# A fused encoder block in fp32 on one core: the up projection with the activations stationary and 512 weight columns moving

## The reference

```python
h = rms_norm(x, norm_mix)                 # x: 256 tokens x 2048
proj = h @ w_in                           # attention: a sliding-window group with sinks
...                                       # and a forgetting-attention group
x = x + mixed @ w_o                       # w_o: 2048 x 2048
h = rms_norm(x, norm_ffn)
u = h @ w_up                              # w_up: 2048 x 11264 (gate half, value half)
c = conv_b + sum(pad(u)[:, j:j + S] * conv_w[j] for j in range(3))    # causal, over tokens
gate, val = c[..., :5632], c[..., 5632:]
x = x + (silu(gate) * val) @ w_down       # w_down: 5632 x 2048
out = rms_norm(x, norm_final)
```

## Time and profile before

| | |
|---|---|
| median of 3 runs | 1058.93 us (1058.59 to 1066.37) |
| the profiled execution | 1067.34 us, span 1065.5 us |
| granted TensorE clock, mean | 0.999 of 2.4 GHz |
| TensorE busy | 1055.5 us |
| VectorE, ScalarE busy | 807.4 us, 627.8 us |
| up projection on TensorE | 332.1 to 831.8 us |

### The profile page before, as it was taken

The page is one execution under the profiler, slowest core; times in us unless marked ns, Lnnn a source line. Parts: engine busy times, 40 slices in busy tenths (PEclk is TensorE's granted clock), DMA queues, the critical chain, the costliest instruction groups (busy, mean ns, idle before and its releaser), DMA issues.

```text
span 1065.5 us, 17821 instructions
## 1 busy us (share of the span) xinstructions
PE 1055.5 (99%) x5921; PEld 902.3 (85%) x5921; DVE 807.4 (76%) x1222; ACT 627.8 (59%) x971; POOL 86.8 (8%) x150
## 2 busy tenths in 40 slices
PE   9999999999999999999999999999999999999997
PEld 8888888888888888888888888888888888888885
DVE  5677777676887777777777777766877888876777
ACT  6957575746455655565555556555655666646663
POOL 1000000001011110111111111101111000000000
PEclk9999999999999999999999999999999999999999
DMA  9575655587888898989898888988889688887993
GB/s 295 177 236 168 183 162 177 177 254 193 255 251 250 261 241 271 245 262 243 257 266 242 264 228 274 258 258 239 249 261 251 218 290 292 279 297 268 329 304 113
DMA packets 191493, 259.35 MB, mean 243 GB/s; under 512 B 10820, under 2 KB 140580, under 8 KB 191328
## 3 DMA queue, kind: packets, MB, share of 16 engines
q1 hardware_dynamic: 173776, 215.32, 62.5%
q0 software_dynamic: 17360, 43.22, 18.4%
q10 hardware_dynamic: 320, 0.34, 0.1%
HBM read 256.73 MB, written 44.06 MB: 282 GB/s over the span
## 4 chain that ended last, share of the span: by engine, by line
PE 92%; DVE 4%; DMA 2%; ACT 1%; issue 0%; SPq 0%; DVEq 0%; ACTq 0%
PE pj L1619 16%; PE tr_ps L1619 15%; PE pj L1377 9%; PE pj L1621 8%; PE tr_ps L1621 8%; PE pj L1379 5%; PE pj L1365 4%; PE pj L1367 4%; PE pj L1366 4%; PE sc_ps L1365 4%; PE sc_ps L1367 4%; PE sc_ps L1366 4%; PE pj L1392 3%; DVE split L911 2%; DVE prob L1124 1%; PE pj L1394 1%
## 5 line engine op out<-in xcount | busy, mean ns | idle before, releaser
L911 DVE TENSOR_TENSOR split<-raw,split 128x1024 fp32r<-128x1024 f32 x266 | 321.4, 1222 | 125.9 <-ACT split L593 120.6
L593 ACT ACTIVATE split<-raw 128x1024 fp32r<-128x1024 f32 x260 | 272.0, 1057 | 88.4 <-PE pj L1621 33.1
L1619 PE MATMUL tr_ps<-act_split,split 128*128 128x512 f32 x704 | 250.1, 399 | 0.3 <-DVE act_split L1111 0.3
L1619 PE MATMUL pj<-act_split,split 128*128 128x512 f32 x704 | 249.8, 399 | 0.0
L1621 PE MATMUL pj<-act_split,split 128*128 128x256 f32 x704 | 197.7, 281 | 0.0
L1621 PE MATMUL tr_ps<-act_split,split 128*128 128x256 f32 x704 | 197.7, 281 | 0.0
L1214 DVE TENSOR_TENSOR split<-raw,split 128x1024 fp32r<-128x1024 f32 (+1 forms) x124 | 136.8, 1135 | 38.3 <-ACT split L856 36.3
L1619 PEld LDWEIGHTS tr_ps<-act_split,split 128*128 128x128 f32 x704 | 132.3, 188 | 33.4 <-DVE act_split L1111 0.5
L1619 PEld LDWEIGHTS pj<-act_split,split 128*128 128x128 f32 x704 | 132.3, 188 | 33.4 <-DVE split L911 0.3
L856 ACT ACTIVATE split<-raw 128x1024 fp32r<-128x1024 f32 (+1 forms) x124 | 119.4, 986 | 69.6 <-PE sc_ps L1367 34.7
L1377 PE MATMUL pj<-act_split,split 128*128 128x512 f32 x416 | 147.5, 398 | 0.0
(11 more groups left out here) (243 smaller groups left out, 1525.9 us busy)
## 6 DMA issues: line engine op xcount, KB each, us to landing
raw<-w_up SPq DMA_DIRECT2D x176, 512.0 KB, 5.6
raw<-w_in SPq DMA_DIRECT2D x72, 512.0 KB, 3.8
raw<-w_down SPq DMA_DIRECT2D x68, 512.0 KB, 5.6
t_dram<-w_down POOLq DMA_DIRECT2D x60, 512.0 KB, 6.0
raw<-t_dram SPq DMA_DIRECT2D x40, 512.0 KB, 5.9
raw<-w_o SPq DMA_DIRECT2D x32, 512.0 KB, 5.3
t_dram<-t_dram POOLq DMA_DIRECT2D x40, 256.0 KB, 5.8
raw<-w_down SPq DMA_DIRECT2D x20, 256.0 KB, 5.9
```

Source lines behind the costliest of these rows:

```text
L593: ins = act.activation(hi[:, slot, 0:TILE], raw[:, slot, 0:TILE], ACT.Copy)
L911: dve.tensor_tensor(lo[:, slot, 0:n], raw[:, slot, 0:n], hi[:, slot, 0:n].bitcast(F32), ALU.subtract).then_inc(lo_done, 1)
L1619: pe.matmul(up_banks[v][b], wh[:, c, b * P:(b + 1) * P], act_both(k), start=k == 0, stop=False, skip_group_check=True)
```

## The change

A step of the up projection is now a pair `j` of halves: half `v` = 0 makes 512 gate columns, `v` = 1 the 512 value columns that belong to them. Each half has eight tiles of 2 blocks of input features x 512 columns (`wide`, rows of 2 KB in place of 1 KB). The activations are stationary, and 512 weight columns move, with `mm3` as in the w_o stage, into two banks for the two blocks of tokens; the two halves alternate between two pairs of banks. The result has tokens on the partitions. It is turned in two steps: ScalarE copies each block of 32 partitions to the partitions of the features (`move_blocks`, 16 copies of 32 partitions x 256 elements, in the first three tiles of the next half), and one VectorE transpose of 128 x 1024 turns all 32 x 32 blocks into `ub` (`turn_moved`). Scaling, convolution, SiLU, gate and split follow during tiles 4 to 7 of that next half, with wider instructions for the last four. The addition of two result halves (`up_r`) is gone.

The fourth group of y is now turned by VectorE in squares as the others, in the first tiles of the up projection. `r2b` is filled by two DMAs on ScalarE's queue, a write of the factors to DRAM and a read that spreads them over the partitions. The post-processing of the last half moves into the first six tiles of the down projection, so the sums tiles start later (`SUMS_AFTER`), and the two more raw slots are used from the thirteenth tile on.

```diff
-UP_SPLITS = [[], [4], [5], [6], [], [8], [9], [10]]
-SUMS_AFTER = ((5, 6, 7, 10, 11, 12, 15, 16, 19, 20), (4, 5, 7, 8, 9, 10, 12, 13, 14, 15))
+SUMS_AFTER = ((8, 9, 11, 12, 13, 15, 16, 17, 19, 20), (4, 5, 7, 8, 9, 10, 12, 13, 14, 15))
...
-    return t % RING if t < 2 * RING else (t - RING) % (RING + EXTRA)
+    return t % RING if t < 3 * RING else (t - 2 * RING) % (RING + EXTRA)
...
+MOVES = {0: (0, 6), 1: (6, 11), 2: (11, SIDE * SIDE)}
+def step_of(j, v, per, c):
+    return j * (2 * per) + (v * per + c)
...
+        moved = sb("moved", [P, 4, MT, SIDE, BLOCK])
+        ub = sb("ub", [P, 4, S + 2])
+        conv_o = sb("conv_o", [P, 2, 4, S])
...
         @block.scalar
+            def root_of_squares(s):
+                if s == 1:
+                    act.wait_ge(y2_tot, 1)
+                    act.activation(root2, tot2, ACT.Sqrt, bias=eps, scale=1.0 / D).then_inc(y2_root, 1)
+                if s == 3:
+                    act.wait_ge(r2_s, 1)
+                    act.dma_start(r2_dram.rearrange("m p -> p m"), r2c, allow_slow_non_contiguous=True).then_inc(r2_out, 16)
+                if s == 6:
+                    act.wait_ge(r2_out, 16)
+                    act.dma_start(r2b[:], r2_dram.rearrange("m p -> (m p)").partition_broadcast(P)).then_inc(d_r2, 16)
+            def move_blocks(j, v, first, last, tiles_done):
+                if first == 0:
+                    act.wait_ge(mm_done, tiles_done)
+                    if not (isinstance(j, int) and 2 * j + v == 0):
+                        act.wait_ge(u_s, step_of(j, v, 2, 0))
+                for i in range(first, last):
+                    a, b = divmod(i, SIDE)
+                    rows = up_banks[v][a * BLOCK:(a + 1) * BLOCK].rearrange("p m (w b i) -> p m w b i", w=4, b=SIDE)[:, :, :, b]
+                    ins = act.activation(moved[b * BLOCK:(b + 1) * BLOCK, :, :, a].rearrange("p w m i -> p m w i"), rows, ACT.Copy)
+                if last == SIDE * SIDE:
+                    ins.then_inc(moved_s, 1)
...
+            def finish(j, v, s):
+                if s in MOVES:
+                    move_blocks(j, v, *MOVES[s], step_of(j, v, UP_TILES, T_UP + UP_TILES))
+                if s in (4, 5):
+                    conv_first(j, v, s - 4)
+                if s == 7:
+                    if v == 0:
+                        silu_gate(j)
+                    else:
+                        gated_hi(j)
+            def up_step(j, v, first):
                 for s in range(UP_TILES):
+                    split_hi(step_of(j, v, UP_TILES, T_UP + s + LEAD), (s + LEAD) % RING)
+                    if v == 1:
+                        finish(j, 0, s)
+                    elif not first:
+                        finish(j - 1, 1, s)
...
             for t in range(DOWN_END):
+                if t == 0:
+                    move_blocks(*last_step, 0, half, T_DOWN)
+                if t + LEAD < DOWN_END:
                     down_hi(t + LEAD)
+                if t == 0:
+                    move_blocks(*last_step, half, SIDE * SIDE, T_DOWN)
+                if t == 2:
+                    conv_first(*last_step, 0)
+                    conv_first(*last_step, 1)
+                if t == 5:
+                    gated_hi(UP_PAIRS - 1)
...
         @block.vector
+            def turn_moved(j, v):
+                dve.wait_ge(moved_s, step_of(j, v, 1, 1))
+                st.done(dve.transpose(ub[:, :, 2:S + 2], moved[:].rearrange("p w m a i -> p w (m a i)")))
...
             def up_step(j, v, first):
+                    if not start:
+                        if s == 3:
+                            turn_moved(p, b)
+                        if s == 4:
+                            scale_rows()
+                        if s == 7 and b == 1:
+                            gate(p)
+                    split_lo(step_of(j, v, UP_TILES, T_UP + s + LEAD), (s + LEAD) % RING)
...
+                        if s in (5, 6):
+                            conv_rest(p, b, s - 5)
+                        if s == 7 and b == 1:
+                            gated_lo(p)
...
         @block.tensor
             def up_step(j, v, first):
+                if not first:
+                    pe.wait_ge(moved_s, step_of(j, v, 1, -1))
...
+                    if first and v == 0:
+                        pe.wait_ge(ylo_s, 2 * s + 2)
+                    pe.wait_ge(lo_done, step_of(j, v, UP_TILES, T_UP + s + 1))
+                    wh, wl = wide(hi, s % RING), wide(lo, s % RING)
+                    for c in range(2):
+                        k = 2 * s + c
+                        for m in range(MT):
+                            ins = mm3(up_banks[v][:, m], act_hi[:, k, m * P:(m + 1) * P], act_lo[:, k, m * P:(m + 1) * P],
+                                      wh[:, c], wl[:, c], start=k == 0)
```

303 lines of the change are left out of this document (127 added, 176 removed).

## The result

| | median of its runs | profiled execution | its span |
|---|---|---|---|
| before | 1059.56 us (9 runs, 1057.65 to 1068.86) | 1067.34 us | 1065.5 us |
| after | 1071.1 us (9 runs, 1069.57 to 1076.11) | 1069.73 us | 1067.9 us |

The kernel after is slower by a factor of 1.0095, 95% interval 1.0062 to 1.0128: clear of noise, but small. I had forecast 1045 us and a range of 1039 to 1060.

A forecast was written before the change was run, and what follows sets the result against it. The prediction took TensorE, busy for 1055.5 of 1065.5 us, as the bound. It summed -21.0 (faster tiles), +1.1 (stage start) and +6.0 (down projection) to -13.9 us, from a median of 1058.93 to 1045.0 us, range 1039 to 1060.

The forecast's parts named there:

- TensorE's 21.0 us: Up projection: 176 tiles at 2.720 us, 478.7 us in place of 499.7, so 21.0 us less.
- The chain of 43.8 us per pair: Up-projection loop: ScalarE and VectorE steps in sequence take 43.8 us per pair against TensorE's 43.5; no stall counted.
- margin of 4.3 us: Up-projection loop: the split behind the transpose ends about 12 us into the half and is wanted at 16.3.
- Rival (b): Up-projection loop: the chain becomes the bound through the moves' pitch, from 0.42 us on; 1059 to 1090 us, chance 0.10.
- Moves of 0.385 us, no overlap: Up projection, ScalarE: each of sixteen moves per half takes 0.385 us without overlap, 6.2 us per half.
- rival (a): Up projection: the moves overlap and little is given back; 1040 to 1041 us, chance 0.19.
- rival (c): Up projection: TensorE's tile gets no faster, since columns alone count; 1061 us, chance 0.02.
- Start of the stage, +1.1 us: Up projection's start: y's last group turned by VectorE makes TensorE wait 1.1 us, between 0 and 3; row factors hidden.
- Rival (d): Up projection's start: the row factors' way through DRAM holds VectorE, up to 7 us once; 1052 us, chance 0.04.
- Start of the down projection, +6.0 us: Down projection: the last half's post-processing, the tile 12 load and closer sums tiles cost 6.0 us, ends 2 and 12.
- The load of tile 12 behind g_lo: Down projection: tile 12 may be loaded only after g_lo, so TensorE waits 2.8 us, and 0.5 us behind it.
- the mild form of (b): Up-projection loop: move pitch of 0.395 to 0.42 us, 1048 to 1059 us; chance 0.22, shared with a high down start.

The follow-up runs named there:

- e1: The kernel before, unchanged, profiled again to get an execution near 1058 us; 1058.48 us.
- e2: The kernel after with eight moves of 64 partitions per half instead of sixteen of 32, output not the reference's; 1054.26 us.
- e3: The kernel after with SiLU, gate, g_hi and g_lo about half a step later, all work kept; 1058.56 us.
- e9: The kernel after with two more moves in each half, written to PSUM columns that nobody reads; 1086.61 us.
- late gate: SiLU and gate half a step later than in the kernel after; 1058.56 us alone, 1055.46 us with the row factors spread by the matmul.
- e7: The kernel after with late gate, row factors by the matmul, and the extra raw slots used from down-projection tile 17 instead of 13; 1055.95 us.
- e16: The kernel after with the sixteen moves reordered, four with the same target partitions behind each other; 1074.38 us.
- e13: The kernel after with the moved blocks in two free PSUM banks in place of SBUF; 1065.45 us.
- e4: The kernel after with VectorE's wait for the row factors moved to ahead of the first scaling; 1074.14 us.

## Why the prediction was wrong

**TensorE's 21.0 us: the form was right, the reference was wrong.** 0.227 us per matmul and 2.720 us per tile came as forecast. But the 2.826 us of the old tile were read from an execution of the upper group and then subtracted from a median of the lower. I had seen that the profile was 8 us above the median and didn't ask where those 8 us lay; they lay in the very matmuls that the change takes away (e1). With 2.771 us the gain is 10.8 us. This one step is 10.2 us of the miss. The profile of after shows 0.227 us throughout, as the earlier trace rows did, and its nine runs show no second group.

**The chain of 43.8 us per pair ("Within the loop I therefore count no stall").** This is the step that failed in kind: a term put at nothing that was 12.4 us. Measured is 44.90, 21.80 for the gate half and 23.10 for the value half, where I had 21.3 and 22.5. ScalarE's part was 9.42 us (forecast 9.3), VectorE's 11.33 and 11.2 (11.0), SiLU and g_hi 0.97 each (1.0 and 0.95), the gate 1.22 (1.25); the rest, between 0.3 and 0.4 us per pair, are hand-overs between the engines, for which I had nothing. No engine's part was wrong by more than 3 per cent, though one term in it was: the first four convolution steps of the gate half took 1.94 us for my 1.7, 0.26 of it idle between the second and the third. (The load of ScalarE, 17.6 us per half, was added up a little low: by the prices I named, eight splits and four convolution starts are 10.8 us and not 8.2 + 2.2. Nothing hung on it.) What failed is the conclusion: I had two loops of 43.8 and 43.5 us, which was a coin toss within my own error of 1 us, and gave the tie to TensorE because of a margin of 4.3 us. A margin covers a lag once; 1.4 us per pair use it up in three pairs. It cost 12.4 us in the loop. That the circle was the cause, and neither late loads nor the sum of the work, is shown by e2, e3 and e9: it went when the circle got shorter or was opened, and grew with it. Rival (b) named this circle and its price right, but tied it to the moves' pitch ("it decides from 0.42 us on"). The pitch was 0.386 to 0.390, and the circle closed all the same, through the other terms.

**Moves of 0.385 us, no overlap**: right (0.387), and L654 was the right neighbour, so rival (a) is out; rival (c) is out by the 0.227 us. The groups by form of the kernel after:

```profile
L820 ACT ACTIVATE moved<-tr_ps 32x256 f32<-32x256 f32 x176 | 66.2, 376 | 2.5
...
L1197 DVE STREAM_TRANSPOSE ub<-moved 128x1024 f32<-128x1024 f32 x22 | 27.4, 1246 | 17.3 <-ACT moved L820 17.3
```

**Start of the stage, +1.1 us**: the sum was right (1.2), but by luck; its parts weren't. The last block of y cost 0.2 us in the profile of after, and 0.2 to 2.2 us in those of the experiments. The row factors, forecast as hidden at 5.6 us per transfer, took 11.3 us for the 1 KB write and 7.0 for the read, held VectorE for 4.1 us and TensorE for 0.9. Rival (d) was partly true; by the matmul it is worth 2.0 us on the kernel after (1071.1 and 1069.12, within the spread of after) and 3.1 with the late gate.

**Start of the down projection, +6.0 us**: measured 9.9, within the ends of 2 and 12, but in part by luck, since it came out of other parts. "ScalarE is free at T + 0.5" was T + 4.4, since ScalarE enters the stage with what the loop left it behind; tiles 3 and 4 waited 3.3 us, where I had none, and tile 7 waited 1.5 where I had 0.85. Both went or halved with the late gate. The load of tile 12 behind g_lo was to cost 3.3 us; there are 1.4, and they stay when that load waits for nothing (e7), so that step fell. The three waits late in the stage (2.4 us for my 1.2) were placed at single plain tiles and are at gaps of two.

**The account.** Against the execution near 1058 us: TensorE -10.8, start +1.2, loop +12.4, down projection +9.9, an earlier begin of the stage -1.4: +11.3, and the spans differ by 1067.9 - 1056.7 = 11.2. The forecast was -13.9; the 25 us between are 10.2 from the reference, 12.4 from the chain and 3.9 from the down start, less 1.4 of a begin that varies. The range missed since it took in neither the smaller gain nor more than the mild form of (b); each alone would have given 1055 to 1058.

## What to carry to other kernels

When two engines hand a piece of work back and forth, add up the circle, hand-overs too, and compare it with the bound's period: if the two lie within the error of your prices, as 43.8 and 43.5 us did here, count the circle as the bound, for a margin in tiles only postpones the waits. Look first for an order in which neither engine's queue holds the next round behind the other's last result; here that change of order gave 12.5 us with all of the work still done, and sixteen copies per half made 7 per cent cheaper gave 5.7. And where the profiled execution is far from the median, find out in which stage before subtracting anything from either.

## What the runs showed of the hardware

- A 256-column matmul behind a 512-column one started 0.230 us after it in one execution (e1) and 0.236 us in another of the same kernel, over a whole stage and at the same granted clock of 1.00, 9.7 us over 176 tiles; the 512-column form alone stayed at 0.227. What selects the group isn't settled.
- ScalarE's copies of 32 partitions x 256 elements with other source or target partitions than the copy before didn't overlap: 0.386 to 0.390 us apart into SBUF (after, e16), 0.361 into PSUM (e13); with the partitions of the copy before, into PSUM, 0.285 to 0.303 (e9). The Trainium skill ("Perfetto Trace Analysis", section "Optimizing Scalar/DVE Operations") gives ScalarE a data-access overhead per instruction of about 93 ns on SBUF and 51 on PSUM. All of these copies read PSUM, so only the place written differs; the trace has the sign of that, with 26 ns between the two pitches in place of 42.
- A DMA of 1 KB from SBUF to DRAM in pieces of 4 bytes landed after 11.3 us, more than twice the 5.0 us (median) of a 512 KB weight tile in the same kernel; in six experiments that kept it (e2, e3, e4, e9, e13, e16) it was 8.5 to 11.3.
- With the SiLU only inside the loop (e3 and the other kernels with the late gate) two table loads of 1.28 us stand in each pair, where the kernel after has one for its SiLUs in all; the difference in the code is that after writes its first SiLU ahead of the loop. That this is the reason was not tried.
